# Three transformer blocks on one core: the merge of the dilations put inside the first gated projection, with new norm sums and another order in the mixers

## The chip, the cores and the metric

The kernel runs on one NeuronCore of one Trainium2 chip. Its time is the device time of one launch in microseconds (us); lower is better. The kernel before takes 5122.53 us, the median of 3 runs (5117.61 to 5122.73).

Work that is spoken of here runs on TensorE (PE, with its weight loads as PEld), VectorE (DVE), ScalarE (ACT) and GpSimd (POOL). SyncE (SP) issues most DMAs; ACT issues some (ACTq). x in on-chip memory is 128 partitions by 8 chunks of channels by 1024 tokens. An accumulator bank holds 128 x 512 values of fp32.

## The reference

Three blocks in series on x of 1024 tokens by 1024 channels, all in fp32. The first mixes four groups (sparse attention, differential attention, retention, a state-space scan), the second is an RWKV group, a convolution and a feed-forward, the third is this hybrid layer:

```python
def mixture_of_dilations(q, k, v):
    slopes = alibi_slopes_3(N_HEADS_B)
    outs, lses = [], []
    for _, dilation in PATTERNS:
        o, l = dilated_window_attention(q, k, v, dilation, slopes)
        outs.append(o)
        lses.append(l)
    w = jax.nn.softmax(jnp.stack(lses, axis=0), axis=0)
    o = jnp.stack(outs, axis=0)
    return jnp.sum(w[..., None].astype(o.dtype) * o, axis=0)

def hybrid_layer(x, w_in, b_gate, g_pre, g_post, ln_g, ln_b, w_s, b_s, w_pa, w_pb, w_o):
    h = rms_norm_3(x, g_pre)
    proj = h @ w_in
    u_a, v_a, z_a, q_b, k_b, v_b, z_b, gate_a, gate_b = jnp.split(proj, SPLIT_OFFS, axis=-1)
    y_a = spatial_gating(jax.nn.gelu(u_a), jax.nn.gelu(v_a), ln_g, ln_b, w_s, b_s) * jax.nn.silu(z_a)
    y_b = mixture_of_dilations(q_b.reshape(hs), k_b.reshape(hs), v_b.reshape(hs)).reshape(B, S, D_B)
    y_b = y_b * jax.nn.silu(z_b)
    ...
    m = g_a * (y_a @ w_pa) + g_b * (y_b @ w_pb)
    return x + rms_norm_3(m @ w_o, g_post)
```

## The kernel before

Every large product goes through `dense`. To keep fp32 accuracy both operands are split into a high half (rounded by ACT to TensorE's fp32r format) and a low half (the rest), and each product is three matmuls: high by high, high by low, low by high. A block of weights is 1024 x 256 (or 512) values. SP loads it in four DMAs (L119), ACT rounds it (L127), POOL takes the rest (L136), and PE multiplies it with the split activations: four banks a block, 24 matmuls of 512 columns a bank (L243). In the projections of the third block DVE copies or adds each finished bank into x (`write_columns`, `close_gate`). Weights are double-buffered, and the first block of the next `dense` is loaded and rounded under the last block of this one (`upcoming`). Each `dense` and each stage is a program block of its own, and all engines meet at its end.

The tail of the third block is a series of such stages: the first spatial gating, `proj_a0` (half of y_a @ w_pa), the second spatial gating, `proj_a1` (the other half, closed with gate a, whose rows ACT loads at L3315), `merge_dilations`, `proj_b` (closed with gate b), `split_columns` "m", which splits x for the last product, `proj_o`, and `norm_in_place`. `merge_dilations` (L3176) goes over 8 tiles of 128 tokens. It loads the three dilations' rows of a tile (128 x 3 x 8 heads x 130: 128 outputs, the denominator and the exponent) and the gate rows z, makes the softmax weights of the three on DVE and ACT, multiplies and adds on DVE (L3227 to L3232) and POOL (L3249, the third dilation), gates (L3234), turns the tile on PE (L3261), and splits the result into `yb`'s halves.

Four norms are late (`LateNorm`): the product's first block is made with x unnormed, in eight chunks over all eight banks, while ACT squares the chunks and PE sums them (L440: eight matmuls a chunk, each with a 128 x 128 piece of the square as the stationary operand and one or two columns moving). The sums then become scales, which PE spreads over the partitions (L449). These are `norm1` at the start of the program, `norm2`, `norm2b` (before the feed-forward) and `norm3`. The one of the program's start also loads x.

The mixers of the first block (retention, the scan, and the end of all four groups) go over 8 tiles. PE's order in a tile is score, segments, turn, retain, carry, and `turn_mixed` of the tile before, which turns the eight 128 x 128 parts of the mixed result (L1485). DVE's order in a tile is written out as calls at L1761 and following. The order within an engine is always the order of the code; there is no planner.

## Time and profile before

| quantity | value |
| --- | --- |
| median of 3 runs | 5122.53 us |
| profiled execution | 5127.73 us |
| its span | 5126.1 us |
| mean granted TensorE clock | 0.91 of full |
| PE busy | 4392.3 us (86%) |
| PEld busy | 3629.6 us (71%) |
| DVE busy | 1864.7 us (36%) |
| ACT busy | 1286.4 us (25%) |
| POOL busy | 1082.2 us (21%) |
| DMA | 403.70 MB, mean 79 GB/s |

The span is the part of the profiled execution between its first and its last instruction; 1.6 us of the execution lie outside it. Busy shares are means over the whole program: PE is busy nearly all the time in the dense products and much less in the stages between them.

### The profile page before, as it was taken

The page shows a single profiled execution, that of the slowest core. Times are in us where ns is not written, and L with a number is a line of the kernel's source. Part 1 is how long each engine was busy: PE and PEld are TensorE (multiplying, and loading weights), DVE is VectorE, ACT ScalarE, POOL GpSimd, SP SyncE. Part 2 cuts the span into 40 slices and gives each one's busy share as a digit, 9 for nine tenths or more (in the row PEclk, how much of TensorE's full clock was granted, in tenths as well). Part 3 has the DMA queues.
Part 4 walks back from the last instruction along what each step waited for, and adds up shares of the span by engine and source line. Part 5 has one row for each costly group of instructions (what it writes and reads, how often), then busy time and mean ns, then how long its engine had stood idle before and what let it go on. Part 6 is the DMA issues. An engine that isn't in the chain of part 4 may idle for free. (4 is left out here: it accounts for less than half of the span.)

```text
span 5126.1 us, 56677 instructions
## 1 busy us (share of the span) xinstructions
PE 4392.3 (86%) x22018; PEld 3629.6 (71%) x22018; DVE 1864.7 (36%) x3205; ACT 1286.4 (25%) x2204; POOL 1082.2 (21%) x544
## 2 busy tenths in 40 slices
PE   7997878749993888579999999999899999889277
PEld 6886667648772878457887877888788888667265
DVE  3021565661375665224234324000133333314532
ACT  3120323332213444211000012112244444311111
POOL 1120001231231655211222212212111111122120
PEclk9997889868996999888999999999999999787588
DMA  2333111221233110211111112232333333423422
GB/s 100 107 132 84 36 24 36 79 71 46 104 113 132 36 38 24 79 42 40 51 41 50 50 42 80 103 129 87 87 95 109 94 95 95 140 66 126 132 78 78
DMA packets 268404, 403.70 MB, mean 79 GB/s; under 512 B 52597, under 2 KB 179446, under 8 KB 262650
## 3 DMA queue, kind: packets, MB, share of 16 engines
q1 hardware_dynamic: 222330, 308.97, 19.8%
q10 hardware_dynamic: 43632, 86.53, 4.5%
q0 software_dynamic: 2192, 4.80, 0.4%
q8 instruction: 166, 2.72, 0.2%
q14 instruction: 84, 0.69, 0.0%
HBM read 281.46 MB, written 118.75 MB: 78 GB/s over the span
## 5 line engine op out<-in xcount | busy, mean ns | idle before, releaser
L136 POOL TENSOR_TENSOR weights_wlow<-weights_raw,weights_whigh 128x1024 fp32r<-128x1024 f32 (+1 forms) x236 | 664.2, 2834 | 2668.2 <-ACT weights_whigh L127 2668.0
L243 PE MATMUL acc<-h_high_half,weights_whigh 128*128 128x512 f32 x1440 | 569.9, 396 | 95.9 <-POOL weights_wlow L136 67.7
L127 ACT ACTIVATE weights_whigh<-weights_raw 128x1024 fp32r<-128x1024 f32 (+1 forms) x236 | 267.7, 1163 | 1359.8 <-PE acc L243 740.7
L243 PE MATMUL acc<-h_high_half,weights_wlow 128*128 128x512 f32 x1440 | 568.2, 395 | 0.0
L243 PE MATMUL acc<-h_low_half,weights_whigh 128*128 128x512 f32 x1440 | 567.5, 394 | 0.0
L243 PEld LDWEIGHTS acc<-h_high_half,weights_whigh 128*128 128x128 f32 x1440 | 275.4, 191 | 158.6 <-POOL weights_wlow L136 74.0
L3102 PE MATMUL acc<-h_high_half,weights_whigh 128*128 128x512 f32 x768 | 332.4, 433 | 0.0
L243 PEld LDWEIGHTS acc<-h_low_half,weights_whigh 128*128 128x128 f32 x1440 | 275.1, 191 | 58.0
L243 PEld LDWEIGHTS acc<-h_high_half,weights_wlow 128*128 128x128 f32 x1440 | 275.3, 191 | 57.6
L246 PE MATMUL acc<-weights_whigh,h_high_half 128*128 128x512 f32 x768 | 303.3, 395 | 14.0 <-PEq L187 14.0
L3102 PE MATMUL acc<-h_low_half,weights_whigh 128*128 128x512 f32 x768 | 302.9, 394 | 0.0
L246 PE MATMUL acc<-weights_wlow,h_high_half 128*128 128x512 f32 x768 | 302.4, 394 | 0.0
L246 PE MATMUL acc<-weights_whigh,h_low_half 128*128 128x512 f32 x768 | 302.2, 394 | 0.0
L3102 PE MATMUL acc<-h_high_half,weights_wlow 128*128 128x512 f32 x768 | 301.6, 393 | 0.0
L1789 DVE TENSOR_TENSOR x_here<-x_here,acc 128x512 f32<-128x512 f32 x96 | 66.0, 688 | 500.5 <-PE acc L243 500.5
L243 PE MATMUL acc<-hidden_high,weights_whigh 128*128 128x512 f32 x512 | 202.1, 395 | 12.4 <-PEq L187 12.4
L243 PE MATMUL acc<-hidden_high,weights_wlow 128*128 128x512 f32 x512 | 201.8, 394 | 0.0
L3009 DVE SCALAR_TENSOR_TENSOR gated_biased_sb<-gated_near_ends_sb,gated_slope_sb,acc 128x384 f32<-128x384 f32 x40 | 24.6, 614 | 434.3 <-PE acc L2966 434.3
L246 PEld LDWEIGHTS acc<-weights_whigh,h_high_half 128*128 128x128 f32 x768 | 146.6, 191 | 46.1 <-issue 15.5
L3102 PEld LDWEIGHTS acc<-h_high_half,weights_whigh 128*128 128x128 f32 x768 | 146.3, 191 | 31.3
L246 PEld LDWEIGHTS acc<-weights_whigh,h_low_half 128*128 128x128 f32 x768 | 146.3, 191 | 31.2
L246 PEld LDWEIGHTS acc<-weights_wlow,h_high_half 128*128 128x128 f32 x768 | 146.6, 191 | 30.4
(533 smaller groups left out, 8344.4 us busy)
## 6 DMA issues: line engine op xcount, KB each, us to landing
weights_raw<-w_cols SPq DMA_DIRECT2D x94, 512.0 KB, 5.0
weights_raw<-w_ff SPq DMA_DIRECT2D x64, 512.0 KB, 3.9
weights_raw<-w_rows SPq DMA_DIRECT2D x30, 1024.0 KB, 7.0
att<-gated_result_sb SPq DMA_DIRECT2D x96, 130.0 KB, 2.2
merge_o_sb<-att SPq DMA_DIRECT2D x24, 520.0 KB, 5.5
weights_raw<-w_out SPq DMA_DIRECT2D x24, 512.0 KB, 3.7
cols<-cols1p_out ACTq DMA_DIRECT2D x40, 256.0 KB, 2.1
rows<-rows1p_out ACTq DMA_DIRECT2D x32, 256.0 KB, 2.7
```

What stands on the lines that cost most here:

```text
L127: self.core.nc.scalar.activation(high[p][:, half * (KC // 2):(half + 1) * (KC // 2), :], raw[half], ACT.Copy).then_inc(self.core.sem("roun ...
L136: self.core.nc.gpsimd.tensor_tensor(low[p][:, hs, :], raw[half], high[p][:, hs, :].bitcast(F32), ALU.subtract).then_inc(self.core.sem("wei ...
L243: mm = nc.tensor.matmul(core.acc[b][:, :], wt[p][:, k, c * P:(c + 1) * P], h[:, k, half * HALF:(half + 1) * HALF], start=first, stop=final)
L246: mm = nc.tensor.matmul(core.acc[b][:, 0:width], h[:, k, b * P:(b + 1) * P], wt[p][:, k, :], start=first, stop=final)
L1789: return core.nc.vector.tensor_tensor(to, to, acc, ALU.add)
L3009: nc.vector.scalar_tensor_tensor(out=biased, in0=mask, scalar=self.slope[p][:, st["dilation"]:st["dilation"] + 1], in1=acc, op0=ALU.mult, ...
L3102: mm = nc.tensor.matmul(core.acc[b][:, :], wt[n % 2][:, k, c * P:(c + 1) * P], of[:, k, half * HALF:(half + 1) * HALF], start=(k == 0 and ...
```

## The change

It touches four places.

1. The merge of the dilations has no stage of its own any more. A class `Merge` runs inside `proj_a0` beside the matmuls: tile by tile, PE turns a tile before a given bank (`TURNED_AT`), DVE makes the weights and the sums of a tile before it copies a given bank (`SUMMED_AT`), POOL gates tiles after the rest of a block's weights (`GATED_AFTER`), ACT makes the first dilation's part, issues the loads of tiles 2 to 7 and stores the turned tiles as rows `yb` in DRAM. They are loaded again during `proj_a1`.
2. `proj_b` and `proj_o` get a `source`: their activations are split chunk by chunk, high on ACT and low on DVE, while the first block multiplies chunk by chunk over its four banks.
3. In `LateNorm` a square is the moving operand and the column of ones (or gains) the stationary one, so that a chunk's sums are two matmuls of 512 columns; the row of sums is then turned back by eight transposes (`turn`). The first block starts when its weights are rounded, before their rest is there, and its order is high by high, low by high, high by low. At the start of the program the loads of x are issued after the first weights block instead of after two. The third block's matmuls no longer wait for every copy of the second.
4. In the mixers `turn_mixed` comes two tiles later, and DVE's and ACT's calls are reordered; two squares go from DVE to ACT, where the root's table is loaded ahead of time.

```diff
@@ -202,7 +204,8 @@
             if late:
                 for it in range(there, 2):
                     load(it, 0, it)
-                late.sync(sp)
+                    if it == 0:
+                        late.sync(sp)
...
+                if source and it == 0:
+                    for b in range(nb):
+                        pe.wait_ge(emptied[b], at[f"emptied_{b}"])
+                    for k in range(KC):
+                        pe.wait_ge(arrived[0], at_arrived + k + 1)
+                        through_banks(0, k, 0, high, whigh)
+                        through_banks(0, k, 1, high, wlow)
+                        pe.wait_ge(arrived[1], at_arrived + k + 1)
+                        through_banks(0, k, 2, low, whigh)
+                    return
                 for b in range(nb):
-
-                    pe.wait_ge(emptied[b], it + at[f"emptied_{b}"])
+                    if merge:
+                        merge.tensor_at(pe, it, b)
...
-                pe.wait_ge(split, at["weights_split"] + 2)
+                pe.wait_ge(core.sem("rounded"), at["rounded"] + 2)
                 for b in range(8):
                     pe.wait_ge(emptied[b], at[f"emptied_{b}"])
-                late.clear_sums(pe)
+                late.wait(pe, "ready", 1)
                 for k in range(KC):
                     late.wait(pe, "highs", k + 1)
                     through_banks(0, k, 0, high, whigh)
-                    through_banks(0, k, 1, high, wlow)
                     late.wait(pe, "lows", k + 1)
-                    through_banks(0, k, 2, low, whigh)
+                    through_banks(0, k, 1, low, whigh)
+                    if k == 0:
+                        pe.wait_ge(split, at["weights_split"] + 2)
+                    through_banks(0, k, 2, high, wlow)
                     if k < KC // 2:
                         late.sums(pe, 2 * k)
                         late.sums(pe, 2 * k + 1)
+                    if k == KC // 2:
+                        late.turn(pe)
...
+                        nc.vector.tensor_tensor(low[:, k, :], source(k), high[:, k, :].bitcast(F32), ALU.subtract).then_inc(arrived[1], 1)
                 for b in range(1 if empties == 2 else 0, nb, empties):
+                    if merge:
+                        merge.vector_at(v, it, b)
...
+                        if brought_by:
+                            brought_by(a, k)
+                        nc.scalar.activation(high[:, k, :], source(k), ACT.Copy).then_inc(arrived[0], 1)
...
     def sums(self, pe, k):
 
         n = self.n
         self.wait(pe, "squared", k + 1)
+        for h in range(2):
+            mm = self.core.nc.tensor.matmul(self.core.acc[4 + h][0:n, :], self.per[:, k, :], self.squares[k % 4][:, h * HALF:(h + 1) * HALF],
+                                            start=k == 0, stop=k == KC - 1)
+        mm.then_inc(self.sem("summed"), 1)
+
+    def turn(self, pe):
+
+        n = self.n
+        self.wait(pe, "rows", 2)
         for t in range(NT):
-            mm = self.core.nc.tensor.matmul(self.core.acc[4][:, n * t:n * t + n], self.squares[k % 4][:, t * P:(t + 1) * P],
-                                            self.per[:, k, :], start=False, stop=True, skip_group_check=True)
-        mm.then_inc(self.sem("summed"), 1)
+            mm = self.core.nc.tensor.transpose(self.core.acc[6][:, n * t:n * t + n], self.squares[2][0:n, t * P:(t + 1) * P],
+                                               self.core.ident[0:n, 0:n])
...
+                    if t >= 2:
+                        turn_mixed(t - 2)
...
+                    act(sq[:, 0:MIX], dif[:, :], ACT.Square)
+                    act(sq[:, MIX:2 * MIX], ro[f % 2][:, :], ACT.Square).then_inc(sig("squared"), 1)
+                    if f:
+                        a.wait_ge(sig("warm_exp"), f)
+                    act(warm[:, :], core.eps[:, :], ACT.Sqrt).then_inc(sig("warm"), 1)
...
                     if t < NT:
                         scores(t)
+                        steps_in(t)
                     if t >= 2:
                         rest(t - 2)
-                    if t < NT:
-                        steps_in(t)
                     if t:
                         centre(t - 1)
+                        statistics(t - 1)
                     if t < NT:
                         within(t)
-                    if t:
-                        statistics(t - 1)
-                    if t < NT:
                         renew(t)
                         outputs(t)
-                        if t + 1 < NT:
-                            widen(t + 1)
+                    if t:
+                        sums(t - 1)
+                    if t + 1 < NT:
+                        widen(t + 1)
                     if t:
                         mix(t - 1)
                 rest(NT - 1)
...
-                    tt(t0[:, :, :], o[p][:, 0, :, 0:AE], bc(w[:, 0, :], AE), ALU.mult)
-                    then(tt(t1[:, :, :], o[p][:, 1, :, 0:AE], bc(w[:, 1, :], AE), ALU.mult))
-                    tt(t0[:, :, :], t0[:, :, :], t1[:, :, :], ALU.add).then_inc(sig("two"), 1)
...
+    TURNED_AT = {3: 0, 5: 1, 6: 2, 8: 3, 9: 4, 11: 5, 12: 6, 14: 7}
+    SUMMED_AT = {0: 0, 1: 1, 3: 2, 4: 3, 6: 4, 7: 5, 9: 6, 10: 7}
+    GATED_AFTER = {1: (0, 1), 2: (2, 3, 4), 3: (5, 6, 7)}
...
+    def sync(self, sp, first):
+
+        if first:
+            self.load(sp, 0)
+            self.load(sp, 1)
+        else:
...
+        if t == 0:
+            self.exponents(v, 0)
+        v.wait_ge(sig("weights"), t + 1)
...
+        if t + 1 < NT:
+            self.exponents(v, t + 1)
+        v.wait_ge(sig("first"), t + 1)
+        for i in (1, 2):
+            for h in range(AH):
+                ins = nc.vector.scalar_tensor_tensor(out=self.t[p][:, h, :], in0=self.o[p][:, i, h, 0:AE], scalar=self.w[p][:, i, h:h + 1],
+                                                     in1=self.t[p][:, h, :], op0=ALU.mult, op1=ALU.add)
+            if i == 1:
+                self.then(v, ins)
+        ins.then_inc(sig("summed"), 1)
+
...
+    def pool_after(self, pool, it):
+
+        for t in self.GATED_AFTER.get(it, ()):
+            p = t % 2
+            pool.wait_ge(self.sig("summed"), t + 1)
+            pool.wait_ge(self.sig(f"loaded{p}"), 64 * (t // 2 + 1))
+            if t >= 2:
+                pool.wait_ge(self.sig("turned"), t - 1)
+            self.core.nc.gpsimd.tensor_tensor(self.y[p][:, :, :], self.t[p][:, :, :], grouped(self.z[p][:, :], AE), ALU.mult
+                                              ).then_inc(self.sig("gated"), 1)
...
+        pe.wait_ge(self.sig("gated"), t + 1)
+        if t >= 2:
+            pe.wait_ge(self.sig("taken"), t - 1)
+        for k in range(AH):
+            mm = self.core.nc.tensor.transpose(self.core.acc[4 + 2 * (t % 2) + k // 4][:, (k % 4) * P:(k % 4 + 1) * P],
+                                               self.y[t % 2][:, k, :], self.core.ident[:, :])
+        mm.then_inc(self.sig("turned"), 1)
...
+    def take(self, a, t):
+
+        p, act = t % 2, self.core.nc.scalar.activation
+        a.wait_ge(self.sig("turned"), t + 1)
+        if t >= 2:
+            a.wait_ge(self.sig(f"stored{p}"), 16 * (t // 2))
+        for h in range(2):
+            ins = act(self.out[p][:, 4 * h:4 * h + 4, :], self.core.acc[4 + 2 * p + h].rearrange("p (k t) -> p k t", k=4), ACT.Copy)
+        ins.then_inc(self.sig("taken"), 1)
+        a.wait_ge(self.sig("taken"), t + 1)
+        a.dma_start(self.core.d["yb"][:, t * P:(t + 1) * P].rearrange("(k p) t -> p k t", p=P), self.out[p][:, :, :]
+                    ).then_inc(self.sig(f"stored{p}"), 16)
+
+    def emptied(self, a, it, b):
+
+        t, act = 2 * it + b // 2, self.core.nc.scalar.activation
+        p = t % 2
+        if t >= 1 and t + 1 < NT:
+            a.wait_ge(self.sig("gated"), t)
+            self.load(a, t + 1)
+        a.wait_ge(self.sig("shares"), t + 1)
+        if t >= 2:
+            a.wait_ge(self.sig("gated"), t - 1)
+        for h in range(AH):
+            ins = act(self.t[p][:, h, :], self.o[p][:, 0, h, 0:AE], ACT.Copy, scale=self.w[p][:, 0, h:h + 1])
+        ins.then_inc(self.sig("first"), 1)
+        if t + 1 < NT:
+            a.wait_ge(self.sig("exponents"), t + 2)
+            act(self.w[1 - p][:, :, :], self.w[1 - p][:, :, :], ACT.Exp).then_inc(self.sig("weights"), 1)
+        if t >= 2:
+            self.take(a, t - 2)
+
+    def scalar_last(self, a):
...
+                y = split_pair(core, c2, "y")
+                spatial_gating(core, 0, sums, less, rstd, *y, weights)
+                with Stage(core, "merge") as st:
+                    dense(core, "proj_a0", y, d["w3_pa"], 0, 4, 256, empty=write_columns(core, x), empties=1,
+                          weights=weights, upcoming=(d["w3_pa"], 4, 256), aside=Merge(core, st))
+                spatial_gating(core, 1, sums, less, rstd, *y, weights)
+                gates_in = c2.enter_context(nc.sbuf_tensor("gates_in", [P, KC, SEQ], F32))
+                c3 = c2.enter_context(ExitStack())
+                yb = c3.enter_context(nc.sbuf_tensor("yb_in", [P, KC, SEQ], F32))
+                gates = Gates(core, gates_in, d["gates3"][0:D, :], (yb, d["yb"]))
+                dense(core, "proj_a1", y, d["w3_pa"], 4, 4, 256, empty=close_gate(core, x, gates, True), empties=1,
+                      weights=weights, upcoming=(d["w3_pb"], 0, 256), aside=gates)
+                gates = Gates(core, gates_in, d["gates3"][D:2 * D, :])
                 dense(core, "proj_b", y, d["w3_pb"], 0, 4, 256, empty=close_gate(core, x, gates, False), empties=1,
-                      weights=weights, upcoming=(d["w3_out"], 0, 256), aside=gates)
...
+                      weights=weights, upcoming=(d["w3_out"], 0, 256), aside=gates,
+                      source=lambda k: yb[:, k, :], brought_by=lambda a, k: a.wait_ge(core.sem("yb_loaded"), 16 * KC))
+                c3.close()
+                dense(core, "proj_o", y, d["w3_out"], 0, 4, 256, empty=write_columns(core, x), empties=1, weights=weights,
+                      source=lambda k: x[:, k, :])
```

How the order on the engines moves. On PE in the mixers, around the end of one tile; `mix_mixed_sb` is the mixed result that is turned. Before:

```order
L1462 MATMUL acc<-mix_S_sb,mix_xbc_sb 128x128 x2
L1466 MATMUL acc<-mix_xdd_sb,mix_xb_sb 128x128 x2
L1472 MATMUL acc<-mix_xdt_sb,mix_M_sb 128x64 x4
L1485 MATMUL acc<-ident_here,mix_mixed_sb 128x128 x8
L1404 MATMUL acc<-mix_q_sb,mix_k_sb 128x128 x4
L1413 MATMUL acc<-mix_late,ident_here 128x512
L1416 MATMUL acc<-mix_tri,mix_spread_sb 128x128 x4
```

and now:

```order
L1513 MATMUL acc<-mix_xdt_sb,mix_M_sb 128x64 x4
L1447 MATMUL acc<-mix_q_sb,mix_k_sb 128x128 x4
L1456 MATMUL acc<-mix_late,ident_here 128x512
L1459 MATMUL acc<-mix_tri,mix_spread_sb 128x128 x4
L1469 MATMUL acc<-ident_here,mix_xbc_sb 128x128 x4
L1474 MATMUL acc<-mix_xbc_sb 128x128 x2
L1525 MATMUL acc<-ident_here,mix_mixed_sb 128x128 x8
```

The scores, segments and turns of the next tile now stand ahead of the transposes of a mixed tile, and that tile is one older.

On DVE in the merge, the second half of one tile; `merge_t_sb` is the weighted sum, `merge_o_sb` the loaded rows, `merge_w_sb` the weights. Before:

```order
L3226 TENSOR_TENSOR merge_w_sb<-merge_w_sb,merge_den_sb 128x24
L3211 REGISTER_ALU
L3227 TENSOR_TENSOR merge_t_sb<-merge_o_sb,merge_w_sb 128x1024
L3228 TENSOR_TENSOR merge_t_sb<-merge_o_sb,merge_w_sb 128x1024
L3211 REGISTER_ALU
L3229 TENSOR_TENSOR merge_t_sb<-merge_t_sb 128x1024
L3232 TENSOR_TENSOR merge_t_sb<-merge_t_sb,merge_o_sb 128x1024
L3234 TENSOR_TENSOR merge_y_sb<-merge_t_sb,merge_z_sb 128x1024
```

and now, inside `proj_a0`, where L3691 copies a bank:

```order
L3298 TENSOR_TENSOR merge_w_sb<-merge_w_sb,merge_den_sb 128x24
L3271 TENSOR_TENSOR merge_top_sb<-merge_o_sb 128x8
L3272 TENSOR_TENSOR merge_top_sb<-merge_top_sb,merge_o_sb 128x8
L3274 TENSOR_TENSOR merge_w_sb<-merge_top_sb,merge_o_sb 128x8 x3
L3306 SCALAR_TENSOR_TENSOR merge_t_sb<-merge_o_sb,merge_w_sb,merge_t_sb 128x128 x16
L3691 COPY x_here<-acc 128x512
L3294 TENSOR_TENSOR merge_ws_sb<-merge_w_sb,merge_o_sb 128x24
```

The exponents of the next tile (L3271 to L3274) stand ahead of the sums of this one (L3306), and a bank's copy stands behind both.

On ACT in the same stage, where before stood only the rounding of weights (L127). Now:

```order
L3340 ACTIVATE merge_w_sb<-merge_w_sb 128x24
L127 ACTIVATE weights_whigh<-weights_raw 128x1024 x2
L3366 ACTIVATE merge_t_sb<-merge_o_sb,merge_w_sb 128x128 x8
L3370 ACTIVATE merge_w_sb<-merge_w_sb 128x24
L3251 DMA merge_o_sb<-att 128x8x130 x3
L3253 DMA merge_z_sb<-rows 128x1024
L3366 ACTIVATE merge_t_sb<-merge_o_sb,merge_w_sb 128x128 x8
L3370 ACTIVATE merge_w_sb<-merge_w_sb 128x24
L127 ACTIVATE weights_whigh<-weights_raw 128x1024 x2
```

The first dilation's part of tile 0 (L3366) stands behind the rounding of the second block's weights, and the loads of tile 2 stand behind the whole of tile 0.

## Rows read from the trace of the kernel before

**Rows 1.** PE's waits over the span: releaser, us in total, times, longest.
```profile
PE acc L3261 <- DVE merge_y_sb L3234: 104.5, 8, 21.5
```

**Rows 2.** Timeline at the tail's joins: start, us, what, [idle before it, releaser].
```profile
4783.87 1.97 PE L3261 MATMUL acc<-ident_here,merge_y_sb 128*128 128x128 f32 x8 [21.55 <-DVE merge_y_sb L3234]
4885.50 0.77 PE L243 MATMUL acc<-yb_high_half,weights_whigh 128*128 128x512 f32 x1 [2.97 <-PEq L591]
4987.35 0.77 PE L243 MATMUL acc<-m_high_half,weights_whigh 128*128 128x512 f32 x1 [13.00 <-PEq L591]
```

**Rows 3.** Timeline: the gates' loads, the end of proj_a1, and the merge's first loads.
```profile
4672.94 4.21 ACTq L3315 DMA_DIRECT2D gates_a<-gates  x8
4762.36 0.69 DVE L3338 TENSOR_TENSOR x_here<-x_here,acc 128x512 f32<-128x512 f32 x1 [4.03 <-PE acc L243]
4764.48 2.25 SPq L3195 DMA_DIRECT2D merge_o_sb<-att  x3
```

**Rows 4.** Timeline of proj_a0: first matmul, last copy, rounding of the second block.
```profile
4511.16 0.77 PE L243 MATMUL acc<-ya_high_half,weights_whigh 128*128 128x512 f32 x1 [5.94 <-PEq L591]
4601.11 0.69 DVE L3583 COPY x_here<-acc 128x512 f32<-128x512 f32 x1 [4.75 <-PE acc L243]
4535.83 2.01 ACT L127 ACTIVATE weights_whigh<-weights_raw 128x1024 fp32r<-128x1024 f32 x2 [18.68 <-PE acc L243]
```

**Rows 5.** Timeline of the merge: first exponent of tile 0, POOL's third dilation.
```profile
4773.49 0.17 DVE L3216 TENSOR_TENSOR merge_top_sb<-merge_o_sb 128x8 f32<-128x8 f32 x1 [9.72 <-DMA merge_z_sb<-rows]
4793.23 1.90 POOL L3249 TENSOR_TENSOR merge_o_sb<-merge_o_sb,merge_w_sb 128x1024 f32<-128x1024 f32 x1 [11.93 <-DVE merge_t_sb L3229]
```

**Rows 6.** Window: us, busy PE, PEld, DVE, ACT, POOL, PEclk, DMA share, GB/s.
```profile
4780.00:4782.00 2.00, 0.00 (x0) 0.00 (x0) 0.67 (x1) 0.00 (x0) 1.30 (x1) 0.50 0.00 0
```

**Rows 7.** Timeline of the mixers: operations of the new merge's kinds and sizes.
```profile
1032.79 1.13 ACT L1582 ACTIVATE mix_seg_sb<-acc,mix_ncs_sb 128x128 f32<-128x128 f32 x4
1039.51 0.46 DVE L1726 SCALAR_TENSOR_TENSOR mix_state_sb<-mix_state_sb,mix_fade,acc 128x64 f32<-128x64 f32 x2
```

**Rows 8.** Windows of the late norms' stretches, columns as in rows 6.
```profile
22.20:99.00 76.80, 72.35 (x324) 60.64 (x324) 35.88 (x32) 30.30 (x31) 11.03 (x4) 0.87 0.22 80
1245.10:1322.50 77.40, 72.93 (x329) 60.73 (x329) 39.06 (x39) 30.45 (x32) 11.03 (x4) 0.84 0.15 52
2306.50:2381.80 75.30, 71.13 (x324) 59.80 (x324) 29.44 (x31) 23.63 (x25) 13.51 (x6) 0.83 0.13 41
3064.10:3138.40 74.30, 69.78 (x329) 58.26 (x329) 39.04 (x39) 29.23 (x31) 11.07 (x4) 0.88 0.17 56
```

**Rows 9.** Timeline: norm3's first sums and first ordinary matmul; the last norm's squares.
```profile
3067.01 4.59 PE L440 MATMUL acc<-norm_per,norm_square 128*128 128x2 f32 x32
3138.39 0.77 PE L243 MATMUL acc<-h_high_half,weights_whigh 128*128 128x512 f32 x1 [4.46 <-DVE cols3p_out L311]
5087.46 1.06 ACT L657 ACTIVATE post_tmp_sb<-x_here 128x1024 f32<-128x1024 f32 x1 [0.66 <-PE acc L669]
```

**Rows 10.** Timeline of the program's start: the second weights block, the first x chunk.
```profile
5.26 11.38 SPq L119 DMA_DIRECT2D weights_raw<-w_cols  x4
21.02 1.15 ACT L457 ACTIVATE h_high_half<-x_here,norm_gains 128x1024 fp32r<-128x1024 f32 x1 [8.51 <-DMA x_here<-xT]
```

**Rows 11.** Timeline and a window of the mixers, PE and DVE.
```profile
1003.61 1.97 PE L1485 MATMUL acc<-ident_here,mix_mixed_sb 128*128 128x128 f32 x8 [7.78 <-DVE mix_mixed_sb L1756]
1126.22 1.97 PE L1485 MATMUL acc<-ident_here,mix_mixed_sb 128*128 128x128 f32 x8 [6.95 <-DVE mix_mixed_sb L1756]
...
1028.09 0.69 DVE L1669 TENSOR_TENSOR mix_inner_sb<-acc,mix_decay 128x512 f32<-128x512 f32 x1 [3.77 <-PE acc L1404]
1037.94 0.94 DVE L1717 TENSOR_TENSOR mix_sq_sb<-mix_dif_sb 128x256 f32<-128x256 f32 x1
1131.64 0.42 DVE L1717 TENSOR_TENSOR mix_sq_sb<-mix_dif_sb 128x256 f32<-128x256 f32 x1
...
1044.00:1064.40 20.40, 11.10 (x74) 9.89 (x74) 13.81 (x31) 6.88 (x15) 9.04 (x11) 0.75 0.33 103
```

256 lines of the change are left out of this document (116 added, 140 removed).

## The prediction, made blind

> **What bounds the kernel now.** The page first: PE is busy 86% of a span of 5126.1 us, no other engine over 36%, so time is to be had where PE waits. PE's waits say where: the longest entry is the merge of the dilations, 104.5 us in 8 waits for DVE [rows 1]. Then the timeline at the joins, to see what stands between the dense products. The merge begins when `proj_a1`'s last matmul ends (4762.3) and ends with `proj_b`'s first (4885.50), 123.2 us; the split of `m` leaves PE idle 13.0 us [rows 2, 3]. In the mixers PE is busy 11.1 us of a period of (1126.22 - 1003.61) / 6 = 20.4 us, and waits about 7.8 us a tile for DVE, which is itself busy 13.8 us [rows 11]. In the late norms PE is busy nearly all the time, but with many tiny matmuls and at a granted clock of 0.83 to 0.88 [rows 8, 9]. Inside `proj_a0` PE never waits: 4511.16 to 4601.1 is 89.9 us, sixteen banks of 4.75 + 0.69 = 5.44 us and 2.9 us more, since the first matmuls, behind a wait, run at TensorE's lower level of 1.2 GHz (the first is 0.77 us long) [rows 4]. So DVE, ACT and POOL have room there.
>
> All durations come from the profiled execution, 5127.73 us, which lies 5 us above the median of the runs. I sum against it and take off the 5 us at the end.
>
> **The tail: merge and splits.** What goes: the merge stage, 123.2 us, and the split of `m`, 13.0 us [rows 2]. What comes at the two joins: the barrier, from `proj_a1`'s last matmul to the first instruction of the next stage, 4762.3 to 4764.48 = 2.2 us [rows 3]. In front of `proj_b` ACT first issues eight gate loads, 4.2 us [rows 3], and only then splits its first chunk, 1.05 us (a 128x1024 activation [rows 9]): 7.5 us. In front of `proj_o` it is 2.2 + 1.05 = 3.3 us. The later chunks are split at 1.05 us each, while PE takes 12 matmuls, half a bank's 5.44 = 2.7 us, per chunk, so they are hidden. One more program block closes, 1 us.
>
> What `proj_a0` pays is the disputed term. The merge's work of a tile now sits in the queues of DVE, ACT and POOL, in a chain: load; exponents on DVE; weights; the first dilation on ACT; 16 fused multiply-adds on DVE; the gate on POOL; eight transposes on PE. Pieces:
> - Load: in the merge stage the first exponent came 4773.49 - 4764.48 = 9.0 us after the first issue [rows 3, 5], and from 4780 the DMA engines stood still [rows 6], so the second tile had landed by +15.5.
> - First dilation on ACT: four 128x128 activations with a scale took 1.13 us, so eight take 2.3 [rows 7].
> - DVE: two multiply-adds of 64 columns took 0.46 [rows 7], 0.23 each; 16 are 3.7 us. This is a lower bound, at 128 columns they may be longer.
> - POOL's gate: 1.9 us, from its product of the same size [rows 5].
>
> Start: SP issues tiles 0 and 1 ahead of the second block's weights, which so land at about +19 us; ACT rounds them for 2.0 us [rows 4] and only then makes tile 0's first part (it stands behind the rounding), to 23.3; DVE to 27, POOL to 29. PE wants tile 0 before bank 3, at 2.9 + 3 x 5.44 = 19.2 us, and waits 10.
>
> Steady state: there are two buffers, so ACT issues the load of tile t+1 only when tile t-1 is gated. DVE makes the exponents of t+1, and so waits for that load, before the sums of tile t, and POOL can gate t only after those. So nothing overlaps the load: 9.0 + 0.8 (the small exponents and weights) + 3.7 + 1.9 = 15.4 us a tile, 15.6 with handshakes. PE would need a tile in 1.5 to 2 banks, 8 to 11 us. So PE goes at the chain's pace: tile 0 at 29, tile 5 at 29 + 5 x 15.6 = 107 us. Tile 6 is late once more: ACT rounds the weights of the last block, which PE's bank 11 (at 114.5) sets free, ahead of its load, so 2 + 9 + 0.8 + 3.7 + 1.9 after 114.5 is 132; tile 7, whose load is in by then, at 139; two banks follow: 152 us in place of 89.9, **+62 us**. Bounds: were all of it hidden, PE would pay only 64 transposes, 8 x about 1.2, less than the 1.97 that eight take behind a wait [rows 11], +10 us; with loads slowed by the weights and by the stores of `yb` (10.5 us and more) +80.
>
> The Trainium skill (DMA: Bandwidth & Descriptors, Specifications) gives about 358 GB/s as the limit of HBM for a core; by it a tile of 2.1 MB would land in 5.9 us, and the stage would be some 20 us shorter than I say. The measured 9.0 us for the same tile stands in rows 3 and 5 and decides.
>
> Tail: -123.2 + 7.5 - 13.0 + 3.3 + 62 + 1 = **-62 us** (bounds -114 and -44).
>
> **The late norms.** Stretches from the first matmul to the first ordinary one: 76.8, 77.4, 75.3 and 74.3 us [rows 8]. New, for two columns: eight chunks over two weight blocks are 16 x 2.72 = 43.5 us; the sums, two matmuls a chunk: in the last norm such a pair came every 1.06 + 0.66 = 1.72 us [rows 9], and eight pairs are 13.8 us, against 18.4 for four groups of 32 tiny ones at 4.59 us [rows 9]; the spread is four such matmuls, 3.4, for two columns and two, 1.7, for one; the turn 2 and the rest 0.5, estimates of small operations: 63.2 us, and 61.5 with one column. The 4.46 us in which PE waited for the copies of the second block [rows 9] goes, and with it the restart at the lower clock behind it, 2.8 us (as the 2.9 above), which lies outside the stretches. So norm3 saves 74.3 + 2.8 - 63.2 = 13.9, norm2 17.0, norm2b 75.3 + 2.8 - 61.5 = 16.6, norm1 76.8 - 61.5 = 15.3. At the start ACT waited 8.51 us for x behind the second block's weights, whose issue took 11.38 us [rows 10]; x now goes first, 8.5 us. Sum 71; I take **-70**. Bounds: -30, if the sums, whose stationary operand is one or two columns wide, run at the lower clock as the tiny ones did; -75.
>
> **The mixers.** A period of 20.4 us holds 3.77 us in which DVE waits for PE's scores [rows 11]: PE stands in `turn_mixed` for the tile before, which waits for DVE. This circle is cut, since the turned tile is two old and the scores stand ahead of it. Two squares of 0.94 us leave DVE [rows 11]. 20.4 - 3.8 - 1.9 = 14.7 us. What is late next is DVE, at 13.8 - 1.9 = 11.9 busy us plus its waits for PE and ACT; PE has 11.1, POOL 9.0, ACT 6.9 plus two squares of under 1 us and one table load. So 5.7 x 7 tiles = **-40 us**. Bounds: -45 (period 14), and -20, if the squares and the second table load on ACT bring half of the wait back.
>
> The same square took 0.94 us in the middle, where POOL works on its own tile, and 0.42 behind the last, where POOL had done [rows 11]. The Trainium skill (SBUF — State Buffer, on the shared port pair) says that a DVE operation with two inputs in SBUF and a GpSimd operation that reads SBUF exclude each other. The two rows agree. By that rule the wait moves to the next two-input operation when the squares go, and the gain is 2 x 0.42 rather than 1.9 us a tile, 7 us less in all.
>
> **Sum.** -62 - 70 - 40 = -172; 5127.7 - 172 = 4955.7, less 5 for the median: I say 4952 us.
>
> **Rivals.**
> - *The merge is wholly hidden.* For it: DVE is idle 4.75 of 5.44 us a bank [rows 4]. Against it: a tile needs 15 us in series, and there are only two buffers. Then `proj_a0` takes 100 us, and the total is 52 less: 4900. Chance 0.10.
> - *The norms give half.* The granted clock is 0.83 to 0.88 over these stretches [rows 8], and if it stays low in the sums and after them, 35 us are missing: 4987. Against it: but for the eight transposes all matmuls there have 512 columns now. 0.13.
> - *The mixers gain little.* DVE's order puts `steps_in` ahead of `rest`, ACT gets squares and a table load a tile, POOL and DVE collide; the period stays near 19: 4985. 0.08.
> - *Slower than before.* The merge's loads are 520-byte rows that share the DMA engines with the weights, and the stores of `yb` and the loads stand in one queue of ACT. Each load delays the next tile one for one, seven times. The gain of 172 is gone when a tile's load takes 172 / 7 = 25 us more than 9.0: from **34 us** on the kernel is slower. The stage before loaded tiles while nothing else moved, so rows don't exclude a doubling (18 us: 5015), but for a fourfold time nothing speaks. 0.03, of which 0.02 slower.
> - *My own case*, near 4952 (4925 to 4985): 0.66.
>
> The measurement tells 0.2%, 10 us, from no change. Faster 0.97, same 0.01, slower 0.02. The range takes in the bounds: below, 5122.5 - 114 - 75 - 45 = 4889, above, 5122.5 - 44 - 30 - 20 = 5029; not all go one way, so 4905 to 5010.
>
> **What would show it.** Right: in `proj_a0`'s place a stretch of about 150 us, in which PE waits some 60 us for POOL at the transposes, at intervals of 15 us; the idle ahead of `proj_b` 7.5 us and ahead of `proj_o` 3.3; late stretches of 61 to 63 us, and the first at 13.7 us instead of 22.2; transposes of the mixed tile without a wait and a period under 15 us. Wrong: `proj_a0` near 100 us or over 170; a wait for weights in `proj_a1`, where 16 DMA issues now stand ahead of ACT's rounding; a late stretch over 68 us; a mixers' period over 17 us, with DVE waiting for ACT at the sums.

## The result

The changed kernel takes 4991.68 us (median of 4 runs, 4988.84 to 4992.33), the kernel before 5122.63 us beside it (5117.61 to 5125.02). The ratio is 0.9745, with a 95% interval of 0.9728 to 0.9761: 131 us less. Forecast were 171 us less, 4952 us, in a range of 4905 to 5010. The profiled execution took 4992.33 us, its span is 4990.6 us, 135.5 us under the span before; the mean granted clock went from 0.91 to 0.926.

The two timelines, cut at the same first matmuls, give where the time went:

| stretch | before | after | difference | forecast |
| --- | --- | --- | --- | --- |
| start to norm1's first matmul | 22.2 | 13.8 | -8.4 | -8.5 |
| norm1's to the mixers' first score | 954.2 | 943.0 | -11.1 | -15.3 |
| mixers, to the first matmul of the product behind | 176.3 | 146.0 | -30.3 | -40 |
| from there to norm2b's first | 1153.8 | 1141.0 | -12.8 | -17.0 |
| norm2b's to norm3's first | 757.7 | 743.0 | -14.7 | -16.6 |
| norm3's to proj_a0's first | 1447.0 | 1429.6 | -17.4 | -13.9 |
| proj_a0 and the second gating | 162.0 | 244.7 | +82.7 | +62 and a closing 1 |
| proj_a1 (and merge) to proj_b's first | 212.4 | 96.6 | -115.8 | -115.7 |
| proj_b's to proj_o's first | 101.9 | 94.3 | -7.5 | -9.7 |
| the rest | 138.8 | 138.6 | -0.2 | 0 |

The start and the joins came out as forecast, the last join 2 us short. Two terms carry the miss of 37 us between the profiled executions: proj_a0 is 20 us worse, the mixers are 10 us worse; the norms lack 6. Between the medians the miss is 40 us, because the forecast took off 5 us from the profiled execution to the median, and here they lie 0.65 us apart.

PE's waits of the changed kernel (releaser, us in total, times, longest), which answer to [rows 1]:

```profile
PE acc L3333 <- POOL merge_y_sb L3320: 57.1, 6, 16.9
...
PE acc L1525 <- DVE mix_mixed_sb L1813: 12.5, 3, 7.7
```

The merge, PE's longest wait before, is now its second longest, at 57 us in place of 104.5, inside proj_a0 and for POOL's gate. The three waits for the mixed tile are those of the first and of the last two tiles; the tiles between have none. The joins, in the timeline of PE and DVE, as [rows 2, 4]:

```profile
4416.49 0.77 PE L260 MATMUL acc<-y_high_half,weights_whigh 128*128 128x512 f32 x1 [5.94 <-PEq L634]
...
4588.12 0.69 DVE L3691 COPY x_here<-acc 128x512 f32<-128x512 f32 x1 [4.75 <-PE acc L260]
...
4757.73 2.04 PE L271 MATMUL acc<-y_high_half,weights_whigh 128*128 128x512 f32 x4 [7.54 <-ACT y_high_half L392]
...
4852.04 1.58 PE L271 MATMUL acc<-y_high_half,weights_whigh 128*128 128x512 f32 x4 [2.95 <-ACT y_high_half L392]
```

proj_a0 is 171.6 us from its first matmul to the start of its last copy, against 89.95. The idle ahead of proj_b is 7.54 us (7.5 forecast) and ahead of proj_o 2.95 (3.3).

One tile of the merge in steady state, tile 3's load and then tile 2's sums, over ACT's queue, DVE, POOL and PE:

```profile
4464.16 2.34 ACTq L3251 DMA_DIRECT2D merge_o_sb<-att  x3
4466.53 1.62 ACTq L3253 DMA_DIRECT2D merge_z_sb<-rows  x1
...
4475.78 0.17 DVE L3271 TENSOR_TENSOR merge_top_sb<-merge_o_sb 128x8 f32<-128x8 f32 x1 [6.48 <-DMA merge_z_sb<-rows]
...
4476.57 4.42 DVE L3306 SCALAR_TENSOR_TENSOR merge_t_sb<-merge_o_sb,merge_w_sb,merge_t_sb 128x128 f32<-128x128 f32 x16
...
4481.06 2.34 POOL L3320 TENSOR_TENSOR merge_y_sb<-merge_t_sb,merge_z_sb 128x1024 f32<-128x1024 f32 x1 [12.23 <-DVE merge_t_sb L3306]
...
4483.45 1.97 PE L3333 MATMUL acc<-ident_here,merge_y_sb 128*128 128x128 f32 x8 [12.70 <-POOL merge_y_sb L3320]
```

It is the chain that was forecast, link by link: the load (issued 4464.16, usable 4475.78, 11.6 us), exponents 0.8, sums 4.42, gate 2.34. The gates end at 4447.3, 4464.1, 4483.4, 4501.2, 4517.7, 4537.1, 4562.8 and 4573.2. From tile 0 to tile 5 that is 89.9 us, 18.0 a tile, where the forecast had 15.6.

The late norms' windows (us, busy PE, PEld, DVE, ACT, POOL, PEclk, DMA share, GB/s), as [rows 8], and norm3's sums, as [rows 9]:

```profile
13.83:78.25 64.42, 64.01 (x236) 40.74 (x237) 32.45 (x28) 30.20 (x32) 14.63 (x6) 1.00 0.28 107
1195.27:1260.75 65.48, 64.92 (x240) 40.82 (x241) 34.96 (x35) 30.50 (x33) 11.04 (x4) 0.97 0.17 61
2243.85:2306.89 63.04, 62.96 (x236) 40.38 (x237) 25.27 (x27) 22.76 (x25) 10.53 (x4) 0.97 0.15 49
2986.87:3050.78 63.91, 63.35 (x240) 39.96 (x241) 34.98 (x35) 29.11 (x32) 11.07 (x4) 1.00 0.19 65
```

```profile
2990.22 3.60 PE L471 MATMUL acc<-norm_square,norm_per 128*2 128x512 f32 x8
```

Forecast were 61.5 and 63.2 us. The granted clock is 0.97 to 1.00 where it was 0.83 to 0.88, so the fear that sums with a stationary operand of one or two columns stay at the lower level (1.2 GHz) did not come true. What was left out of the forecast stands at the start of a stretch: behind the wait for its first chunk norm1's first three groups of four matmuls take 2.05, 1.91 and 2.04 us, its later ones 1.20, 1.07 and 1.07, which is 2.7 us.

```profile
13.83 2.05 PE L271 MATMUL acc<-h_high_half,weights_whigh 128*128 128x512 f32 x4 [13.83 <-ACT h_high_half L497]
...
29.41 1.20 PE L271 MATMUL acc<-h_high_half,weights_whigh 128*128 128x512 f32 x4
```

norm3's first three groups take 1.16, 1.20 and 1.07 us, and its stretch is the one that comes nearest to its forecast.

The mixers in a window of five periods, from tile 0's transposes to tile 5's:

```profile
983.40:1060.90 77.50, 62.66 (x371) 54.51 (x372) 64.55 (x138) 38.17 (x90) 43.58 (x55) 0.74 0.38 125
```

77.5 us are 15.5 a tile, down from 20.4. DVE is busy 64.55 / 5 = 12.9 us of it (13.8 before [rows 11]) and idle 2.6 (6.6 before).

### The profile page after: what moved, and what is told of

The parts are those of the page before. It is cut to its first block and busy times, and to the rows that moved or that the text cites. A ratio compares the mean times of both kernels' runs of the same rounds, so it can differ in the third digit from the quotient of the medians.

```text
span 4990.6 us, 55840 instructions
## 1 busy us (share of the span) xinstructions
PE 4360.2 (87%) x21658; PEld 3550.6 (71%) x21658; DVE 1858.9 (37%) x3257; ACT 1317.6 (26%) x2305; POOL 1088.0 (22%) x544
## 5 line engine op out<-in xcount | busy, mean ns | idle before, releaser
L127 ACT ACTIVATE weights_whigh<-weights_raw 128x1024 fp32r<-128x1024 f32 (+1 forms) x236 | 267.3, 1163 | 1288.5 <-PE acc L260 660.5
L260 PEld LDWEIGHTS acc<-h_high_half,weights_whigh 128*128 128x128 f32 x1440 | 273.2, 190 | 142.8 <-POOL weights_wlow L136 71.3
L263 PE MATMUL acc<-weights_whigh,h_high_half 128*128 128x512 f32 x768 | 301.8, 393 | 13.9 <-PEq L189 13.9
L260 PE MATMUL acc<-y_high_half,weights_whigh 128*128 128x512 f32 x448 | 180.8, 404 | 12.8 <-PEq L634 11.6
L260 PE MATMUL acc<-y_high_half,weights_wlow 128*128 128x512 f32 x448 | 178.8, 399 | 0.0
L260 PE MATMUL acc<-y_low_half,weights_whigh 128*128 128x512 f32 x448 | 178.0, 397 | 0.0
L263 PEld LDWEIGHTS acc<-weights_whigh,h_high_half 128*128 128x128 f32 x768 | 145.5, 189 | 45.6 <-issue 15.5
```

The lines of the kernel that those rows point to most:

```text
L127: self.core.nc.scalar.activation(high[p][:, half * (KC // 2):(half + 1) * (KC // 2), :], raw[half], ACT.Copy).then_inc(self.core.sem("roun ...
L260: mm = nc.tensor.matmul(core.acc[b][:, :], wt[p][:, k, c * P:(c + 1) * P], h[:, k, half * HALF:(half + 1) * HALF], start=first, stop=final)
L263: mm = nc.tensor.matmul(core.acc[b][:, 0:width], h[:, k, b * P:(b + 1) * P], wt[p][:, k, :], start=first, stop=final)
```

## The experiments

**The three parts, each alone in the kernel before.** The hunks of the diff were sorted by part; nothing else was changed. "b_tail" has `Merge`, the `source=` splits and the new tail, "b_norm" `LateNorm` and its lines in `dense`, "b_mix" the hunks in the mixers:

```diff
# b_norm, its lines in dense
-                late.sync(sp)
+                    if it == 0:
+                        late.sync(sp)
...
+                    pe.wait_ge(emptied[b], it + at[f"emptied_{b}"] - (1 if late and it == 2 else 0))
# b_mix, on PE
-                    if t:
-                        turn_mixed(t - 1)
+                    if t >= 2:
+                        turn_mixed(t - 2)
# b_tail
+                          weights=weights, upcoming=(d["w3_pa"], 4, 256), aside=Merge(core, st))
```

> The kernel before with the change's tail alone (merge inside proj_a0, splits per chunk under proj_b and proj_o, gate and yb rows loaded in proj_a1). The norms and mixers stay as before. By the stage times of the two profiles the tail is worth +82.7 (proj_a0 and the second gating) - 115.8 - 7.5 = -41 us: 5082, and the three parts add up (theory A). Rival B: the parts help each other, since DMA or weights arrive at other times; then the three parts alone don't sum to the 131 us of the whole, and this one is more than 10 us off 5082.

> The kernel before with the late norms' change alone. By the stage times: start 8.4, norm1 12.4, norm2 14.8, norm2b 15.2, norm3 13.1, together -64 us: 5059. Rival: the late norms of this kernel run at a lower clock in other surroundings and give half, 5090.

> The kernel before with the mixers' change alone. By the stage times 176.3 us become 146.0, -30 us: 5092. The forecast had -40; if that was right and something else of the whole took 10 us back, 5082.

Measured against 5125.49 us of before (9 runs): tail 5081.40, ratio 0.9916 (0.9902 to 0.9929); norms 5065.18, 0.9885 (0.9870 to 0.9900); mixers 5090.24, 0.9935 (0.9922 to 0.9949). That is -44, -60 and -35 us. The product of the three ratios is 0.9738, the whole has 0.9745 (0.9728 to 0.9761): the parts add up within these intervals, and each is what the stage times of the whole said, within 5 us. None of the runs shows that a part took time from another.

**One wait put back in the norms ("n_wait").**

```diff
-                    pe.wait_ge(emptied[b], it + at[f"emptied_{b}"] - (1 if late and it == 2 else 0))
+                    pe.wait_ge(emptied[b], it + at[f"emptied_{b}"])
```

> The changed kernel with one wait put back: the third weights block of each late norm waits again for the copies of the second block, not of the first. Theory: each of the four norms idles 4.5 us there and then starts at TensorE's lower clock, which the forecast priced at 2.8 us more, so 4 x 7.3 = 29 us: 5021. Rival: the restart costs nothing beyond the idle time, 4 x 4.5 = 18 us: 5010.

Measured 5011.98 us (4 runs), 20 us over the changed kernel, 21.6 by the spans: 5.4 us a norm, between the two. The wait is back as it was, and behind it stands PE's restart:

```profile
1266.54 0.77 PE L260 MATMUL acc<-h_high_half,weights_whigh 128*128 128x512 f32 x1 [4.47 <-DVE cols2p_out L332]
```

From there to the next product's first matmul (1294.74) are 28.2 us; without the wait it is 25.5 us (1260.75 to 1286.27). So the restart does cost 2.7 us in place; the granted clock is 0.50 over its first 5.5 us (1266.54 to 1272). But from one late stretch to the next (for norm3 to proj_a0), the wait cost 6.2, 5.8 and 6.8 us for norm2, norm2b and norm3, and only 3.5 for norm1. The restart's price is real and smaller over the whole than where it is paid; what gives a part back was not found.

**What sets the pace in proj_a0: four orders.** First DVE's order alone, then the issuing queue alone, then both.

```diff
# m_exp, in vector_at
-        if t + 1 < NT:
-            self.exponents(v, t + 1)
         v.wait_ge(sig("first"), t + 1)
...
         ins.then_inc(sig("summed"), 1)
+        if t + 1 < NT:
+            self.exponents(v, t + 1)
# m_sp: tiles 2 to 7 are loaded by SP, called behind each weights block's loads
+    LOADED_AFTER = {1: (2,), 2: (3, 4, 5), 3: (6, 7)}
+    def sync_after(self, sp, it):
+        for t in self.LOADED_AFTER.get(it, ()):
+            sp.wait_ge(self.sig("gated"), t - 1)
+            self.load(sp, t)
...
-        if t >= 1 and t + 1 < NT:
-            a.wait_ge(self.sig("gated"), t)
-            self.load(a, t + 1)
```

> The changed kernel with one move: DVE makes the exponents of tile t+1 behind the sums of tile t instead of ahead of them. Theory A (the load stands in series with the tile's sums and gate): today a tile takes 10.3 (load) + 0.8 + 4.4 (sums) + 2.3 (gate) = 17.9 us. Then the load overlaps the sums, and ACT's order sets the pace: issue of the next load 4.2, first part 2.4, sums 4.4, gate 2.3 = 13.4 us. 4.5 us less for five or six tiles: -25, 4967. Rival B (the DMA engines or DVE's and POOL's use of memory set the pace, not the order): a tile stays at 17 to 18 us, 4990.

> The changed kernel with the merge's loads of tiles 2 to 7 issued by SP instead of ACT, between the weights blocks. Theory A: with the exponents still ahead of the sums the load stays in series, and ACT's issues were hidden beside it: a tile stays at 17.9 us; only the load of tile 7 no longer stands behind ACT's rounding of the last block's weights, which held it 9.0 us. -9: 4983. Rival C (ACT's 4.2 us of issues a tile are themselves the delay): -4.2 x 6 - 9 = -34, 4958.

> Both moves at once: exponents behind the sums, loads issued by SP. Theory A: a buffer goes load 10.3, exponents 0.8, weights 1.2, first part 2.4, sums 4.4, gate 2.3 = 21.4 us, two buffers in turn: 10.7 us a tile, about the pace at which PE wants them (8.2 to 10.9 and 1.1 for the transposes). -7.2 x 5 - 9 = -45 and up to -55 us: 4937 to 4947, more than the sum of the two moves alone. Rival B: loads that now overlap weights and each other take 15 us and more, and the gain stays under 30 us: over 4962.

Measured: 4989.10, 4988.26 and 4978.93 us (4 runs each, before 5123.77), so -3, -3 and -13 us where -25, -9 and -45 to -55 were expected. The first two differ from the changed kernel by no more than the runs of one kernel do, but proj_a0 with the second gating is 3.2 us shorter in both traces, and 11.6 us in the third. My reading of the result, that only the load stands in series, was wrong as it stood. m_exp came out at the 4990 of its rival: a tile still takes 17.3 us, and PE now waits for ACT's copies of the turned tiles instead of the gate. In ACT's queue these copies and the next load's issue stand behind the exponential of the next tile, which now waits some 7.4 us for DVE's exponents, that is for the sums. DVE's move so left the load behind the sums, by way of ACT:

```profile
4482.57 0.22 ACT L3370 ACTIVATE merge_w_sb<-merge_w_sb 128x24 f32<-128x24 f32 x1 [7.37 <-DVE merge_w_sb L3274]
...
4484.21 4.00 ACTq L3251 DMA_DIRECT2D merge_o_sb<-att  x3
...
4521.82 1.94 PE L3333 MATMUL acc<-ident_here,merge_y_sb 128*128 128x128 f32 x8 [12.51 <-ACT merge_out_sb L3349]
```

In the version with both moves the gates end at 4445.8, 4457.4, 4473.9, 4485.5, 4508.4, 4524.2, 4547.1 and 4558.8: three of the seven steps are 11.6 or 11.7 us, near the 10.7 of theory A, but the others are 16.5, 22.8, 15.8 and 23.0. The timelines of ACT and SP's queue in that version show what is in the two longest:

```profile
4485.56 1.92 SPq L3253 DMA_DIRECT2D merge_o_sb<-att  x3
...
4489.49 1.00 SPq L119 DMA_DIRECT2D weights_raw<-w_pa  x2
...
4496.87 2.23 ACT L127 ACTIVATE weights_whigh<-weights_raw 128x1024 fp32r<-128x1024 f32 x2 [9.49 <-DMA weights_raw<-w_pa]
4499.00 2.43 ACT L3373 ACTIVATE merge_t_sb<-merge_o_sb,merge_w_sb 128x128 f32<-128x128 f32 x8
...
4535.60 2.26 ACT L127 ACTIVATE weights_whigh<-weights_raw 128x1024 fp32r<-128x1024 f32 x2 [9.80 <-PE acc L262]
4537.77 2.43 ACT L3373 ACTIVATE merge_t_sb<-merge_o_sb,merge_w_sb 128x128 f32<-128x128 f32 x8
```

Ahead of the first part of tiles 4 and 6 (L3373) ACT stands at the rounding of a weights block, 9.5 us for its load and 9.8 us for PE, which itself waits for the merge. The wait for PE is in the changed kernel too, 14.59 us ahead of the last rounding, and a rounding also holds tile 0 there. That is a second circle beside the load. The wait for the load is largely the edit's own: SP issues this block (4489.49) behind tile 5's load, which waited for tile 3's gate. In the changed kernel the same rounding waited 1.83 us, for PE; in m_sp two roundings waited 16.0 us each for their weights. So m_sp and m_exp_sp take the load out of ACT's queue and put a new wait into SP's.

Fourth, the rounding is moved behind the tile that it held up, and tile 5's load behind the last block's weights:

```diff
# m_order, on ACT, beside both moves above; LOADED_AFTER = {1: (2,), 2: (3, 4), 3: (5, 6, 7)}
-                if not isinstance(it, int) or it + 1 < blocks:
-                    round_block(a, it + 1, 1 - p)
-                elif upcoming:
-                    round_block(a, it + 1, blocks % 2, upcoming[2])
+                def round_next():
...
+                if not merge:
+                    round_next()
...
                     if aside:
                         aside.emptied(a, it, b + 1)
+                    if merge and b == (2 if it == blocks - 1 else 0):
+                        round_next()
```

> As the run with both moves, and a third: on ACT the first dilation's part of tile 2 x block stands ahead of the rounding of the next block's weights, in the last block that of both tiles (before, the rounding stood ahead and waited 9 to 10 us for weights or for PE, with tiles 0, 4 and 6 behind it); SP loads tile 5 behind the last weights block. Theory D (the pace is broken by ACT's rounding that waits, not by the load alone): tile 0 is gated at about +20 instead of +31, the steps of 22.8 and 23.0 us before tiles 4 and 6 become about 11, and proj_a0 takes 115 to 125 us instead of 172: 4936 to 4946. Rival B (DMA): the 11.6 us steps become 15 and more, and the time stays above 4960.

Measured 4955.49 us (4 runs), ratio to before 0.9672 (0.9656 to 0.9689): 36 us less than the changed kernel, while the two moves without it were worth 13. proj_a0 with the second gating is 207.2 us instead of 244.7, so proj_a0 itself some 134; 115 to 125 was expected. That the pace was held by roundings that wait is shown by the two moves together; they were not run apart, so how much of the 23 us over m_exp_sp belongs to the rounding's place and how much to tile 5's load is open. My size was too good. Part of what was left over stands in POOL's timeline of m_order: tile 0's sums were done by 4437, but its gate stands behind the rest of the weights.

```profile
4438.89 4.65 POOL L136 TENSOR_TENSOR weights_wlow<-weights_raw,weights_whigh 128x1024 fp32r<-128x1024 f32 x2 [21.83 <-ACT weights_whigh L127]
4443.49 2.35 POOL L3335 TENSOR_TENSOR merge_y_sb<-merge_t_sb,merge_z_sb 128x1024 f32<-128x1024 f32 x1
```

**The gate loads behind the splits ("best").**

```diff
-            if aside:
+            if aside and not source:
                 aside.scalar(a)
...
                         nc.scalar.activation(high[:, k, :], source(k), ACT.Copy).then_inc(arrived[0], 1)
+                    if aside:
+                        aside.scalar(a)
```

> The same, and in front of proj_b ACT splits the eight chunks of yb before it issues the eight gate loads, not after. The idle time ahead of proj_b falls from 7.5 to 3.3 us, 4.2 us less than m_order, if the gates still land before the first bank is closed (22 us later). Rival: proj_b's first closing waits for the gates, and the 4 us come back there.

Measured 4951.79 us (4948.79 to 4955.27), 3.7 us under m_order, though the ranges of the two runs overlap. The traces tell them apart: the idle ahead of proj_b is 2.95 us in place of 7.31, and proj_b takes 93.1 us in place of 93.0, so nothing comes back there.

**POOL's order ("best2").**

```diff
+                if merge:
+                    merge.gate(pool, merge.GATED_BEFORE.get(it, ()))
                 weights.rest(pool, at, width, it, p)
...
+    GATED_BEFORE = {1: (0,), 2: (2,)}
+    GATED_AFTER = {1: (1,), 2: (3, 4), 3: (5, 6, 7)}
```

> The version before with one more move, on POOL: the gate of tile 0 stands ahead of the rest of the second weights block, that of tile 2 ahead of the third's. There tile 0's sums were done at 4436.9 and its gate ended at 4445.8, behind 4.65 us of rest and a wait for the rounding; tile 2's sums were done at 4464.9 and its gate ended at 4475.4. Theory E (the chain of the merge sets the end of proj_a0, and what stands ahead of a gate on POOL counts one for one): tile 0 is 6.5 us earlier, tile 2 up to 8, of which the later loads take part back: -8 to -14 us, 4938 to 4944. Rival: the rest of the weights, now later by 2.4 us, holds PE at banks 4 and 8, and DVE's two-input operations wait elsewhere: no change, 4952.

Measured 4944.38 us (5 runs, 4940.95 to 4945.04), ratio to before 0.9646 (0.9633 to 0.9660). That is 7.4 us less, just under the expected 8 to 14, and the fastest version of this study, 47 us under the changed kernel. Tile 0's gate ends 20.4 us behind proj_a0's first matmul in place of 27.0. PE's waits there point to the next limit, ACT's copies of the turned tiles, which no run tests:

```profile
PE acc L3353 <- ACT merge_out_sb L3369: 19.9, 4, 7.0
PE acc L3353 <- POOL merge_y_sb L3340: 2.5, 2, 1.4
```

**The mixers: the squares back on DVE ("x_sq").**

```diff
# on ACT
-                    act(sq[:, 0:MIX], dif[:, :], ACT.Square)
-                    act(sq[:, MIX:2 * MIX], ro[f % 2][:, :], ACT.Square).then_inc(sig("squared"), 1)
# on DVE, at the end of statistics
+                    tt(sq[:, 0:MIX], dif[:, :], dif[:, :], ALU.mult)
+                    tt(sq[:, MIX:2 * MIX], ro[f % 2][:, :], ro[f % 2][:, :], ALU.mult).then_inc(sig("squared"), 1)
```

> The changed kernel, but the mixers' two squares stay on DVE, with the new order otherwise. The forecast's term: 1.9 us a tile, 8 tiles, +15: 5006. Rival (the shared access of DVE and POOL: an operation taken away from DVE beside POOL only passes the wait to the next): 2 x 0.42 us a tile, +7: 4998. Third: DVE isn't what sets the period, then no change, 4991.

Measured 5009.22 us (4 runs), 17.5 over the changed kernel; the mixers from first score to last transposes take 140.1 us in place of 126.8, +13.4. The squares take 0.83 and 0.94 us again:

```profile
1025.80 0.83 DVE L1771 TENSOR_TENSOR mix_sq_sb<-mix_dif_sb 128x256 f32<-128x256 f32 x1
1026.55 0.94 DVE L1772 TENSOR_TENSOR mix_sq_sb<-mix_ro_sb 128x256 f32<-128x256 f32 x1
```

The period is 17.1 us instead of 15.5: 1.6 a tile. Of these DVE is busy 1.3 (14.2 against 12.9) and idle 0.3. The forecast's 1.9 is nearer than the 0.84 of the rival that the wait only moves on, and the period goes with DVE's work. Of the 17.4 us between the two spans 11.8 lie in the mixers' stretch; 6.9 lie behind it, where the edit changes nothing, and stay unexplained.

**The mixers: less work on POOL ("x_pool").** The output lacks two of the three sparse branches.

```diff
-                    then(g.tensor_tensor(heads(t1[:, :]), o[1], bc(gate[2], HD), ALU.mult))
-                    then(g.tensor_tensor(t0[:, :], t0[:, :], t1[:, :], ALU.add))
-                    then(g.tensor_tensor(heads(t1[:, :]), o[2], bc(gate[0], HD), ALU.mult))
-                    then(g.tensor_tensor(t0[:, :], t0[:, :], t1[:, :], ALU.add))
```

> The changed kernel, where POOL in the mixers leaves out the second and third branch of the sparse attention (four of its eleven operations a tile, about 2.8 us); the output lacks them. Theory (DVE's two-input operations wait while POOL's read memory): DVE's product of y and z, the difference and the decay product, 0.84, 0.95 and 0.94 us beside POOL, fall towards 0.42 to 0.48, so DVE is busy 1 to 1.5 us less a tile of 12.9, and the period of 15.5 falls by as much: 8 tiles, -10: 4982. Rival: these operations are long by themselves or for another reason, DVE stays at 12.9 us and the time at 4991.

Measured 4993.84 us, no change; the period fell from 15.5 to 15.0 us and DVE is busy 12.7 us a tile, 12.9 before. This does not decide the question, because POOL's other operations moved up beside the same ones of DVE:

```profile
1018.93 1.44 POOL L1560 TENSOR_TENSOR mix_qx_sb<-mix_q_sb,mix_xi 128x512 f32<-128x512 f32 x1
...
1019.17 1.48 DVE L1764 SCALAR_TENSOR_TENSOR mix_dif_sb<-mix_att_sb,mix_nlam_sb 128x256 f32<-128x256 f32 x1
```

The difference that took 0.95 us in the changed kernel takes 1.48 beside a longer operation of POOL. DVE's operation is the same in both: its length goes with what POOL does at that moment.

## Why the prediction was right, and where it was not

- *The joins and the start.* -115.7 forecast and -115.8 measured for merge stage and join, 7.5 and 7.54 us ahead of proj_b, 22.2 to 13.8 at the start. These came from rows of the same barrier, issues and splits, and needed no new price.
- *proj_a0, +62.* The step was right: the chain load, exponents, sums, gate in series with two buffers, and PE at its pace. It was mis-sized by 20 us, so that the term lies above its own bound of +80, and the stage's 171.6 us just past the 170 that the forecast had named as a sign of being wrong. The total stayed in the range only because the range left room for it. Per tile 18.0 against 15.6 us: the loads took 8.9 to 11.8 us, 10.3 in the mean, instead of 9.0; the sixteen sums 4.42 instead of 3.7 (0.276 us at 128 columns, where the row had 64 [rows 7]; called a lower bound, and then used as the value); the gate 2.34 instead of 1.9. Five tiles make 12 us. A load never came near the doubling to 18 us of the rival in which the kernel is slower. The start was 30.8 us, not 29, and the last tiles and banks took 51 us, not 45.
- *What I missed about it.* The forecast saw ACT's rounding ahead of tile 0's first part and ahead of the last load, and priced each once. It did not see that they are a circle of their own, nearly as long as the load's: with the load out of series the gates still end every 16.9 us in the mean (18.0 before) and the kernel gained only 13 us of the 45 to 55 expected. Part of that is the new wait in SP's queue. Moving the rounding, together with tile 5's load, gave another 23 (m_order against m_exp_sp).
- *The rival that the merge is wholly hidden* is excluded: it had 100 us for proj_a0, and the changed kernel takes 171.6. Even best2 needs 200.3 us for proj_a0 and the second gating, where the rival has 172.
- *The norms, -70.* Measured -64. The new stretches were forecast 0.7 to 2.9 us short each (63.0 to 65.5 against 61.5 and 63.2), the sums being 4 x 3.60 = 14.4 instead of 13.8 us and the start of the stretch being slow, a term that the forecast did not have (2.7 us in norm1); and the wait with its restart is worth 5.4 us a norm over the whole, where the forecast had 7.3 (n_wait). The rival that they give only half is excluded, by b_norm's 60 us and by the granted clock.
- *The mixers, -40.* The circle through `turn_mixed` is cut: DVE's idle time fell by 4.0 us a tile (3.8 forecast). Its busy time fell only by 0.9 where 1.9 was forecast, although the squares are worth 1.6 of the period (x_sq): they were 1.77 of the 13.8 us, so DVE's other operations together take 0.9 us more than before. In the new order other ones of them stand beside POOL. The product of y and z is one, first before, then after:

```profile
1035.98 0.41 DVE L1712 TENSOR_TENSOR mix_y_sb<-mix_y_sb,mix_z_sb 128x256 f32<-128x256 f32 x1
```

```profile
1016.75 0.84 DVE L1763 TENSOR_TENSOR mix_y_sb<-mix_y_sb,mix_z_sb 128x256 f32<-128x256 f32 x1
```

  So the period is 15.5 us and not 14.7 (nor under 15, the forecast's sign), 5 us over the tiles. The forecast had weighed the exclusion of DVE and POOL that the Trainium skill states (SBUF — State Buffer, two separate sides) at 7 us less, and left it out of the sum; the fall of the busy time by 0.9 us is what that reading had (0.84). The rest of the miss is the count: the gain holds for 6.6 periods, not 7, and the wait for weights behind the mixers grew from 15.22 to 17.24 us.

## What to carry to other kernels

Before work is put beside matmuls, write down each engine's whole order for one period, with everything that may wait in it, the roundings of weights too: an instruction that waits holds the chain behind it, and a circle can close through an engine that is idle most of the time. Taking one link out of a circle shows nothing while a second one is closed (here -3 and -3 us alone, -13 together, -36 with the roundings moved too). A move can also open a new wait: loads put into SP's queue held up the weights behind them. And a price taken from a row of half the size is a bound, not a value.

## What the runs showed of the hardware

In the rows here a two-input operation of DVE that starts while a POOL operation with operands in on-chip memory is under way ends only when POOL's has ended, however small it is itself. In the changed kernel's proj_a0, POOL's rest of a weights block (two operations in 4.74 us) and then DVE's sums of eight numbers a partition:

```profile
4464.09 4.74 POOL L136 TENSOR_TENSOR weights_wlow<-weights_raw,weights_whigh 128x1024 fp32r<-128x1024 f32 x2
```

```profile
4464.22 2.27 DVE L3295 TENSOR_TENSOR merge_den_sb<-merge_ws_sb 128x8 f32<-128x8 f32 x1
4466.53 2.32 DVE L3296 TENSOR_TENSOR merge_den_sb<-merge_den_sb,merge_ws_sb 128x8 f32<-128x8 f32 x1
```

The same two take 0.17 us each for the tile before. That POOL lets DVE in between its two operations and not within one agrees with the Trainium skill's rule named above (SBUF — State Buffer, two separate sides). It cost nothing here, since the load of the next tile was later. In m_order, where the chain is tighter, it did: beside POOL's rest and gate the sixteen sums of one tile take 7.64 us, where they otherwise take 4.42.

```profile
4471.74 7.64 DVE L3319 SCALAR_TENSOR_TENSOR merge_t_sb<-merge_o_sb,merge_w_sb,merge_t_sb 128x128 f32<-128x128 f32 x16 [4.50 <-ACT merge_t_sb L3378]
```
